# The final sums of a decoder step: sample rows moved to GpSimd, residual rows of two tiles put into TensorE's banks, half of the reads issued from ScalarE

## The chip, the cores and the metric

The program runs on one core of a Trainium2 chip. The core has a matrix engine (TensorE, PE in the profile), a vector engine (VectorE, DVE), an activation engine (ScalarE, ACT), a general engine (GpSimd, POOL) and a queue engine (SyncE, SP), each with its own stream of instructions; they wait for one another only through semaphores. Sixteen DMA engines move data between the device memory (HBM) and the on-chip memory (SBUF); TensorE writes to eight banks of 128 x 512 floats (PSUM). The metric is the time of one execution on the device, in microseconds (us).

## The reference

One decoder layer over 512 prompt rows and 8 sample rows of width 1024: normalisation, input projection, a gated spatial unit beside dilated attention, output projection; then a mixture of experts, and a last normalisation. The part that the change touches is the end:

```
xp = xp + moe(rmsnorm(xp, ln2_g))      # 512 rows
xs = xs + moe(rmsnorm(xs, ln2_g))      # 8 rows
y_prompt = rmsnorm(xp, lnf_g)          # x / sqrt(mean(x^2) + 1e-6) * g
y_sample = rmsnorm(xs, lnf_g)
```

In `moe` each row goes to two experts of the 32; its result is the sum of the two expert rows, each times its gate.

## The kernel before, in words

The rows lie in five tiles: tiles 0 to 3 hold 128 prompt rows each, tile 4 (`NT - 1`) the 8 sample rows. Nothing plans the order: each engine's stream is written out by hand.

The experts run as a loop over 16 pairs of experts (`work`). GpSimd gathers the rows of a pair, TensorE multiplies, ScalarE and VectorE each copy half of the result, and GpSimd scatters it to `y2_dram` (`expert_rows`) in HBM, by an indirect DMA; `y_landed` counts the scatters that have landed. A second round of the loop stands in a branch that every engine passes and none takes here.

Then come the final sums. SP has by then put `x_end`, the residual rows, and `gain_end`, the last gain, on the chip (L607, L608). When all scatters have landed it reads, tile by tile in `READ_ORDER` (sample first), the first-choice and the second-choice expert rows into `rows` (L615, ten DMAs on one queue). The sums are made in `LAST_ORDER`, sample first:

- For the sample and for tiles 0 and 2, VectorE adds gate x row to the residual row, twice (L1482, L1484). For tiles 1 and 3 (`BY_PE`), TensorE multiplies the rows by diagonal matrices of gates into four banks (L1900), and VectorE adds the banks to the residual rows in halves (L1478).
- ScalarE squares each tile with a running sum over the row (L984), and takes the root (L747). The first root needs a table load.
- VectorE takes the reciprocal (L1492) and multiplies row, reciprocal and gain (L1493); `add_rows` of the next tile stands ahead of `final_norm` of a tile in its stream.
- SP writes each tile out when it is ready (L618), and waits for all.

Between the expert loop and the rows, TensorE runs 100 products without a use (`keep_on`, L1797).

L636 is another place, in the attention over cached keys: GpSimd multiplies keys by a query there, in tiles of 128 x 1536. L1019, L1091 and L1133 are passes of VectorE that run near it, each with two inputs: L1019 and L1091 have both in SBUF, L1133 has one in a bank. L643 is a masking pass of GpSimd with one input, and L883 a square of half a tile by ScalarE with a running sum, as in the change.

Of the kernel before, what the change touches and what calls it, by code (L numbers as in the profile page):

```python
# [77 lines left out]
def rows_of(t):  # L78
    return P if t < NT - 1 else NS
# [84 lines left out]
LAST_ORDER = [NT - 1, 0, 2, 1, 3]  # L164
BY_PE = (1, 3)
# [11 lines left out]
ROOM = [32 - 4 * (i + 1) for i, h in TASKS]  # L177

# [28 lines left out]
def build(nc, x_prompt, x_sample, cache_k, cache_v, ln1_g, w_in, sgu_g, sgu_wt, sgu_w, sgu_bt, sgu_b,  # L207
# [7 lines left out]
    with ExitStack() as ctx:  # L215
# [3 lines left out]
        def sem(name):  # L219
            return ctx.enter_context(nc.semaphore(name))  # L220
# [185 lines left out]
        zeroed = sem("zeroed")  # L406
        diags_set, rows_gated = sem("diags_set"), sem("rows_gated")
# [42 lines left out]
        def down_load(sp, j):  # L450
            sp.dma_start(places[j % SLOTS][:, 2], down_v[:, 2 * j:2 * j + 2, :]).then_inc(down_in[j % SLOTS], 16)

# [3 lines left out]
        def _(sp):  # L456
# [165 lines left out]
        def _(pool):  # L622
# [80 lines left out]
            with pool.If(more > 0):  # L703
                pool.wait_ge(tab_ready, 2)
                with pool.Fori(PAIRS, TOTAL - PAIRS + 1, PAIRS) as base:
                    work(base)
            for s_, n_ in ((out_k, 32), (out_v, 32), (out_s, 16)):
                pool.wait_ge(s_, n_)

        @block.scalar  # L710
        def _(act):
# [269 lines left out]
            for i, t in enumerate(LAST_ORDER):  # L981
                n = rows_of(t)
                act.wait_ge(mixed, i + 1)
                nc.scalar.activation(hflat[0:n, 0:D], x_end[0:n, t, :], ACT.Square, scale=D ** -0.5,  # L984
                                     accum_out=stat[0:n, 24 + t:25 + t]).then_inc(sq3, 1)
                root(sq3, i + 1, stat[0:n, 24 + t:25 + t])

        @block.vector
        def _(dve):
# [431 lines left out]
            step(V.tensor_tensor(gates[:, 1, :], gates[:, 0, :], ex, ALU.mult))  # L1421
# [46 lines left out]
            def add_rows(t):  # L1468

                n = rows_of(t)  # L1470
                xt = x_end[0:n, t, :]
                dve.wait_ge(x_back[t], 16)
                if t in BY_PE:
                    i = BY_PE.index(t)
                    dve.wait_ge(rows_gated, i + 1)
                    for half in range(2):
                        xh = xt[:, half * 512:(half + 1) * 512]
                        ins = V.tensor_tensor(xh, (acc, tp)[i][half][:, :], xh, ALU.add)  # L1478
                    ins.then_inc(mixed, 1)
                    return  # L1480
                dve.wait_ge(rows_in[t], 32)  # L1481
                step(V.scalar_tensor_tensor(out=xt, in0=rows[0:n, t, 0], scalar=gates[0:n, 0, t:t + 1], in1=xt,  # L1482
                                            op0=ALU.mult, op1=ALU.add))
                V.scalar_tensor_tensor(out=xt, in0=rows[0:n, t, 1], scalar=gates[0:n, 1, t:t + 1], in1=xt,  # L1484
                                       op0=ALU.mult, op1=ALU.add).then_inc(mixed, 1)

            def final_norm(i, t):
                n = rows_of(t)
                xt = x_end[0:n, t, :]
                dve.wait_ge(mixed, i + 1)  # L1490
                dve.wait_ge(rooted, 2 * NT + i + 1)  # L1491
                step(V.reciprocal(stat[0:n, 24 + t:25 + t], stat[0:n, 24 + t:25 + t]))  # L1492
                V.scalar_tensor_tensor(out=xt, in0=xt, scalar=stat[0:n, 24 + t:25 + t], in1=gain_end[0:n, :],  # L1493
                                       op0=ALU.mult, op1=ALU.mult).then_inc(y_ready, 1)

            add_rows(LAST_ORDER[0])
            for i in range(1, NT):
                add_rows(LAST_ORDER[i])
                final_norm(i - 1, LAST_ORDER[i - 1])
            final_norm(NT - 1, LAST_ORDER[NT - 1])  # L1500

        @block.tensor
        def _(pe):
# [390 lines left out]
            keep_on(100)  # L1894
            pe.wait_ge(diags_set, 2 * len(BY_PE))
            for i, t in enumerate(BY_PE):
                pe.wait_ge(rows_in[t], 32)
                for half in range(2):
# [59 lines left out]
```

## Time and profile before

| | us |
|---|---|
| median of 3 runs | 441.01 |
| lowest, highest | 438.19, 441.26 |
| span of the profiled execution | 437.3 |
| VectorE busy | 214.6 (49%) |
| ScalarE busy | 150.9 (34%) |
| GpSimd busy | 70.5 (16%) |
| TensorE busy | 397.0 (91%) |

The span is the time from the first to the last instruction of one profiled execution; for that execution there is no other time. The three runs are whole executions, without a profile. Busy times are averages over the whole program; what matters for the change is its last 26 us, from the landing of the last scatter on, and which wait ends last there.

### The profile page before, as it was taken

How to read it: one execution, taken by the hardware profiler on the slowest of the kernel's cores; microseconds unless marked ns; L12 is line 12 of the kernel's file. 1: busy time of each engine (PE TensorE's matmuls, PEld its weight loads, DVE VectorE, ACT ScalarE, POOL GpSimd, SP SyncE). 2: the span in 40 equal slices, each digit the busy share in tenths (PEclk: the TensorE clock that was granted, in tenths of full speed). 3: DMA queues.
4: the chain of work that ended last, by engine and by line, in shares of the span. 5: the costliest groups of instructions: out<-in, count | busy, mean ns of one | idle time of the engine just before them, and what ended most of it. 6: DMA issues, size and time to landing. Idle time of an engine off the chain costs nothing. (4 is left out here: it accounts for less than half of the span.)

```text
span 437.3 us, 6404 instructions
## 1 busy us (share of the span) xinstructions
PE 397.0 (91%) x2466; PEld 211.0 (48%) x2466; DVE 214.6 (49%) x442; ACT 150.9 (34%) x321; POOL 70.5 (16%) x59
## 2 busy tenths in 40 slices
PE   1999998999799999999989998979999999999782
PEld 1454443443244434455533557756555555554551
DVE  2968345799597465455351525741222312222276
ACT  5724122132364455454332435211222312222043
POOL 0000113444350100000000000220323223211000
PEclk9999999899899999999999999788999999999897
DMA  8981530874935133940069994899999999994384
GB/s 290 357 245 49 194 96 0 305 273 135 328 117 194 42 101 124 302 157 1 6 222 411 411 414 174 257 375 396 338 409 414 410 410 407 403 402 169 125 332 192
DMA packets 42323, 109.17 MB, mean 250 GB/s; under 512 B 7864, under 2 KB 8632, under 8 KB 42288
## 3 DMA queue, kind: packets, MB, share of 16 engines
q1 hardware_dynamic: 36000, 94.79, 58.8%
q0 software_dynamic: 5856, 12.81, 7.8%
q10 hardware_dynamic: 432, 1.11, 0.8%
q8 instruction: 22, 0.36, 0.3%
q14 instruction: 13, 0.11, 0.1%
HBM read 100.00 MB, written 16.94 MB: 267 GB/s over the span
## 5 line engine op out<-in xcount | busy, mean ns | idle before, releaser
L1540 PE MATMUL bank<-weights_split,tokens_split 128*128 128x512 f16 (+1 forms) x648 | 151.2, 387 | 2.1 <-DVE x L1260 1.4
L1540 PEld LDWEIGHTS bank<-weights_split,tokens_split 128*128 128x128 f16 (+1 forms) x648 | 61.8, 98 | 81.1 <-issue 12.7
L636 POOL TENSOR_TENSOR big<-big,middle 128x1536 f32<-128x1536 f32 x8 | 27.8, 3469 | 93.9 <-DMA middle<-sample_q 52.3
L1848 PE MATMUL bank<-big,tokens_split 128*64 128x256 f32 x320 | 39.0, 399 | 1.6 <-ACT tokens_split L945 1.6
L1438 DVE TENSOR_TENSOR middle<-bank,middle 128x128 f32<-128x128 f32 x16 | 4.7, 293 | 59.2 <-ACT middle L950 59.2
L1848 PEld LDWEIGHTS bank<-big,tokens_split 128*64 128x64 f32 x320 | 23.9, 143 | 13.7 <-ACT tokens_split L945 2.1
L1019 DVE SCALAR_TENSOR_TENSOR weights_split<-middle,weights_split 128x1024 f16<-128x1024 f32 x16 | 20.8, 1333 | 12.8 <-ACT weights_split L738 12.7
L1797 PE MATMUL bank<-half_consts 128*128 128x256 f16 x186 | 23.8, 294 | 2.9 <-issue 2.9
L1515 PE MATMUL bank<-ident,big 128*128 128x128 f32 (+1 forms) x92 | 14.6, 295 | 12.7 <-DVE big L1029 9.3
L670 POOL DMA_INDIRECT tokens_split<-h_rows,middle x16 | 16.3, 1018 | 59.1 <-PE bank L1837 46.0
L822 ACT ACTIVATE middle<-bank 128x128 f32<-128x128 f32 (+3 forms) x32 | 13.9, 435 | 32.0 <-PE bank L1588 31.8
L1797 PEld LDWEIGHTS bank<-half_consts 128*128 128x128 f16 x186 | 19.3, 106 | 7.3 <-issue 3.8
L950 ACT ACTIVATE middle<-bank 128x128 f32<-128x128 f32 x16 | 4.5, 278 | 52.0 <-PE bank L1848 52.0
L683 POOL DMA_INDIRECT expert_rows<-weights_split,middle x16 | 16.1, 1004 | 38.5 <-DVE weights_split L1445 38.5
L652 POOL DMA_DIRECT2D h_rows<-middle x5 | 2.7, 537 | 121.4 <-ACT middle L912 121.4
L1540 PE MATMUL bank<-weights_split,big 128*128 128x512 f16 x96 | 22.0, 379 | 0.0
L1100 DVE CUSTOM_DVE_ANT_0 middle<-bank,big 128x128 f32<-128x128 f32 (+3 forms) x32 | 15.5, 486 | 12.2 <-PE bank L1580 12.0
L1445 DVE COPY weights_split<-bank 128x512 f32<-128x512 f32 x16 | 11.1, 692 | 20.3 <-PE bank L1867 17.7
L1837 PE MATMUL bank<-ident,tokens_split 128*128 128x128 f32 x128 | 18.1, 286 | 1.9 <-DMA tokens_split<-h_rows,middle 1.9
L1867 PE MATMUL bank<-big,middle 128*64 128x512 f32 x80 | 19.3, 604 | 0.6 <-ACT middle L955 0.6
L1515 PEld LDWEIGHTS bank<-ident,big 128*128 128x128 f32 (+1 forms) x92 | 11.0, 154 | 17.8 <-issue 11.8
L1588 PE MATMUL bank<-ident,middle 128*128 128x128 f32 x80 | 15.2, 288 | 4.1 <-DVE middle L1110 2.7
(199 smaller groups left out, 542.8 us busy)
## 6 DMA issues: line engine op xcount, KB each, us to landing
big<-in_w_gate SPq DMA_DIRECT2D x10, 1024.0 KB, 13.8
big<-in_w_up SPq DMA_DIRECT2D x10, 1024.0 KB, 17.5
big<-in_w_down SPq DMA_DIRECT2D x10, 1024.0 KB, 15.2
middle<-in_w_in SPq DMA_DIRECT2D x16, 512.0 KB, 6.6
big<-in_cache_win_k SPq DMA_DIRECT2D x24, 256.0 KB, 3.9
middle<-in_cache_win_v SPq DMA_DIRECT2D x24, 256.0 KB, 4.6
big<-in_w_out SPq DMA_DIRECT2D x8, 512.0 KB, 8.4
big<-expert_rows SPq DMA_DIRECT2D x8, 512.0 KB, 6.9
```

The source lines that it names most:

```text
L636: nc.gpsimd.tensor_tensor(prod[:, :, :], kring[:, b % 2], qb[:, b % 2, :].unsqueeze(1).to_broadcast([P, NPAT, W]), ALU.mult).then_inc(prod ...
L670: nc.gpsimd.indirect_dma_start(out=xg[:, b, :], out_offset=None, in_=h2_dram, in_offset=bass.IndirectOffsetOnAxis(ap=index, axis=0), bound ...
L683: nc.gpsimd.indirect_dma_start(out=y2_dram, out_offset=bass.IndirectOffsetOnAxis(ap=index, axis=0), in_=yrow[:, b, :], in_offset=None, bou ...
L1019: V.scalar_tensor_tensor(out=wg[:, n % 2, 1, 2 * i:2 * i + 2, :], in0=pieces(n)[i], scalar=W_UP, in1=wg[:, n % 2, 0, 2 * i:2 * i + 2, :], ...
L1100: V.tensor_tensor_reduce(out=sp_sb[:, n % 4, 0:width], in0=sbk[n % 2][:, 0:width], in1=mask[:, (3 - i) * P:4 * P], scale=-SCALE, scalar=3. ...
L1515: ins = T.transpose(tp[bank][:, c * m:(c + 1) * m], src, ident[0:m, 0:m])
L1540: ins = T.matmul(out, (hT if rows is None else rows)[:, high_low, k if rows is None else k - 4, tokens], wg[:, place, part, k, columns], s ...
L1588: ins = T.transpose(ptb[:, j * P:(j + 1) * P], sp_sb[:, n % 4, j * P:(j + 1) * P], ident[:, :])
L1797: T.matmul(sbk[1][:, 0:2 * P], before_h, half_consts[:, :, :], start=True, stop=True)
L1837: ins = T.transpose(sbk[k // 4][:, (k % 4) * P:(k % 4 + 1) * P], xg[:, b, k * P:(k + 1) * P], ident[:, :])
L1848: ins = T.matmul((ptb, ovb)[b][e * CAP:(e + 1) * CAP, 0:2 * FE], xT[:, b, k, e * CAP:(e + 1) * CAP], places[slot][:, 0:2, e, k * FE:(k + 1 ...
L1867: ins = T.matmul((acc, tp)[b][half][e * CAP:(e + 1) * CAP, :], hidT[:, b, e * CAP:(e + 1) * CAP], places[slot][:, 2, e, half * 512:(half + ...
```

## The change

The change touches only the final sums.

- The sample's part moves from VectorE to GpSimd: two products of row and gate (L722), two sums (L728), one product with the gain (L731) and one with the reciprocal (L734), each on 8 x 1024. ScalarE still squares and roots (L1022, L1025), VectorE still takes the reciprocal (`inverse3`, L1542).
- For tiles 1 and 3, TensorE first copies the residual rows into the banks, by a product with the identity (L1965), before the filler products, of which 70 are left; the gated rows are added onto them. VectorE's addition falls away. ScalarE squares the banks in halves and adds the two sums (`square3_banks`), and VectorE's norm reads the banks.
- The second-choice rows are read from ScalarE's queue, the first-choice rows still from SP's (`read_rows`, L463).
- The order is now sample, 0, 1, 2, 3. VectorE makes both sums of tiles 0 and 2 first, with the sample's reciprocal between them, and then the four norms.

VectorE's stream behind the expert loop, before (L1482 and L1484 are the two sums, L1478 the addition from the banks, L1492 and L1493 the norm; `rooted` counts ScalarE's roots):

```order
L1482 SCALAR_TENSOR_TENSOR big<-big,middle 8x1024 [waits rows_in4,x_back4,gain_back]
L1484 SCALAR_TENSOR_TENSOR big<-big,middle 8x1024 [waits vector_step]
L1482 SCALAR_TENSOR_TENSOR big<-big,middle 128x1024 [waits rows_in0,x_back0]
L1484 SCALAR_TENSOR_TENSOR big<-big,middle 128x1024 [waits vector_step]
L1492 RECIPROCAL stat<-stat 8x1 [waits rooted,mixed]
L1493 SCALAR_TENSOR_TENSOR big<-big,stat 8x1024 [waits vector_step]
L1482 SCALAR_TENSOR_TENSOR big<-big,middle 128x1024 [waits rows_in2,x_back2]
L1484 SCALAR_TENSOR_TENSOR big<-big,middle 128x1024 [waits vector_step]
L1492 RECIPROCAL stat<-stat 128x1 [waits rooted,mixed]
L1493 SCALAR_TENSOR_TENSOR big<-big,stat 128x1024 [waits vector_step]
L1478 TENSOR_TENSOR big<-bank0,big 128x512 [waits rows_gated,x_back1]
L1478 TENSOR_TENSOR big<-bank1,big 128x512
```

The same place with the change (L1534 and L1536 are the two sums, L1548 the norm of a tile in SBUF, L1553 that of a tile in banks):

```order
L1534 SCALAR_TENSOR_TENSOR big<-big,middle 128x1024 [waits rows_in0,x_back0,gain_back]
L1536 SCALAR_TENSOR_TENSOR big<-big,middle 128x1024 [waits vector_step]
L1542 RECIPROCAL stat<-stat 8x1 [waits rooted]
L1534 SCALAR_TENSOR_TENSOR big<-big,middle 128x1024 [waits rows_in2,x_back2]
L1536 SCALAR_TENSOR_TENSOR big<-big,middle 128x1024 [waits vector_step]
L1542 RECIPROCAL stat<-stat 128x1 [waits rooted]
L1548 SCALAR_TENSOR_TENSOR big<-big,stat 128x1024 [waits vector_step]
L1542 RECIPROCAL stat<-stat 128x1 [waits rooted]
L1553 SCALAR_TENSOR_TENSOR big<-bank0,stat,big 128x512 [waits vector_step]
L1553 SCALAR_TENSOR_TENSOR big<-bank1,stat,big 128x512
```

The sample's passes are gone from VectorE, except the reciprocal, which now stands ahead of the sums of tile 2.

ScalarE's stream at the same place, with the change (L1022 is the square of a tile in SBUF, L1025 the root, L1033 the square of a bank; the last two rows of a bank's tile add the halves and take the root):

```order
L463 DMA big<-expert_rows 8x1024 [waits y_landed1,y_landed0]
L463 DMA big<-expert_rows 128x1024 x4
L1022 ACTIVATE tokens_split,stat<-big 8x1024 [waits sample_mixed]
L1025 ACT_TABLE_LOAD
L1025 ACTIVATE stat<-stat,epsc 8x1 [waits sq3]
L1022 ACTIVATE tokens_split,stat<-big 128x1024 [waits mixed]
L1025 ACTIVATE stat<-stat,epsc 128x1 [waits sq3]
L1033 ACTIVATE tokens_split,stat<-bank0 128x512 [waits rows_gated]
L1033 ACTIVATE tokens_split,stat<-bank1 128x512
L1038 ACTIVATE stat<-stat,epsc 128x1 [waits sq3]
L1040 ACTIVATE stat<-stat 128x1 [waits sq3]
```

The first square, that of the sample, waits for GpSimd's second sum (`sample_mixed`) where it waited for VectorE (`mixed`); the five reads stand ahead of it.

GpSimd's stream behind its branch, which held nothing before:

```order
L722 TENSOR_TENSOR big<-big,middle 8x1024 [waits gates_ready,rows_in4,x_back4]
L722 TENSOR_TENSOR big<-big,middle 8x1024
L728 TENSOR_TENSOR big<-big 8x1024 [waits sample_gated]
L728 TENSOR_TENSOR big<-big 8x1024 [waits sample_mixed,sample_gated]
L731 TENSOR_TENSOR big<-big 8x1024 [waits sq3,gain_back]
L734 TENSOR_TENSOR big<-big,stat 8x1024 [waits sample_inverse,sample_gained]
```

All six are new there; the fifth waits for ScalarE's square, the sixth for VectorE's reciprocal.

The diff, cut to the code that the text speaks of:

```diff
-LAST_ORDER = [NT - 1, 0, 2, 1, 3]
-BY_PE = (1, 3)
+LAST_ORDER = [NT - 1, 0, 1, 2, 3]
+BY_PE, BY_VECTOR = (1, 3), (0, 2)
...
+def squared3(t):
+    return sum(3 if u in BY_PE else 1 for u in LAST_ORDER[:LAST_ORDER.index(t) + 1])
...
+        def read_rows(eng, t, k):
+            at, n = k * ROWS + t * P, rows_of(t)
+            eng.dma_start(rows[0:n, t, k], y2_dram[at:at + n, :]).then_inc(rows_in[t], 16)
...
             for t in READ_ORDER:
-                n = rows_of(t)
-                for k in range(2):
-                    at = k * ROWS + t * P
-                    sp.dma_start(rows[0:n, t, k], y2_dram[at:at + n, :]).then_inc(rows_in[t], 16)
-            for i, t in enumerate(LAST_ORDER):
-                sp.wait_ge(y_ready, i + 1)
+                read_rows(sp, t, 0)
+            for t in LAST_ORDER:
+                sp.wait_ge(sample_ready if t == NT - 1 else y_ready, max(t + 1 if t < NT - 1 else 1, 1))
...
+            xs_end = x_end[0:NS, NT - 1, :]
+            pool.wait_ge(x_back[NT - 1], 16)
+            pool.wait_ge(rows_in[NT - 1], 32)
+            pool.wait_ge(gates_ready, 1)
+            for k in range(2):
+                row = rows[0:NS, NT - 1, k]
+                nc.gpsimd.tensor_tensor(row, row, gates[0:NS, k, NT - 1:NT].to_broadcast([NS, D]),
+                                        ALU.mult).then_inc(sample_gated, 1)
+            for k in range(2):
+                pool.wait_ge(sample_gated, k + 1)
+                if k == 1:
+                    pool.wait_ge(sample_mixed, 1)
+                nc.gpsimd.tensor_tensor(xs_end, xs_end, rows[0:NS, NT - 1, k], ALU.add).then_inc(sample_mixed, 1)
+            pool.wait_ge(gain_back, 16)
+            pool.wait_ge(sq3, squared3(NT - 1))
+            nc.gpsimd.tensor_tensor(xs_end, xs_end, gain_end[0:NS, :], ALU.mult).then_inc(sample_gained, 1)
+            pool.wait_ge(sample_gained, 1)
+            pool.wait_ge(sample_inverse, 1)
+            nc.gpsimd.tensor_tensor(xs_end, xs_end, stat[0:NS, 24 + NT - 1:24 + NT].to_broadcast([NS, D]),
+                                    ALU.mult).then_inc(sample_ready, 1)
...
+            for b in range(2):
+                act.wait_ge(y_landed[b], 8 * PAIRS)
+            for t in READ_ORDER:
+                read_rows(act, t, 1)
...
+            def square3_banks(t):
+                i = BY_PE.index(t)
+                act.wait_ge(rows_gated, i + 1)
+                for half in range(2):
+                    nc.scalar.activation(hflat[:, half * 512:(half + 1) * 512], (acc, tp)[i][half][:, :], ACT.Square,
+                                         scale=D ** -0.5,
+                                         accum_out=stat[:, 64 + 2 * i + half:65 + 2 * i + half]).then_inc(sq3, 1)
+                act.wait_ge(sq3, squared3(t) - 1)
+                first, both = stat[:, 64 + 2 * i:65 + 2 * i], stat[:, 24 + t:25 + t]
+                nc.scalar.activation(first, first, ACT.Identity, bias=epsc[:, :]).then_inc(sq3, 1)
+                act.wait_ge(sq3, squared3(t))
+                nc.scalar.activation(both, stat[:, 65 + 2 * i:66 + 2 * i], ACT.Sqrt, bias=first).then_inc(rooted, 1)
...
-            add_rows(LAST_ORDER[0])
-            for i in range(1, NT):
-                add_rows(LAST_ORDER[i])
-                final_norm(i - 1, LAST_ORDER[i - 1])
-            final_norm(NT - 1, LAST_ORDER[NT - 1])
+                for half in range(2):
+                    at = slice(half * 512, (half + 1) * 512)
+                    ins = V.scalar_tensor_tensor(out=xt[:, at], in0=(acc, tp)[BY_PE.index(t)][half][:, :],
+                                                 scalar=stat[:, 24 + t:25 + t], in1=gain_end[:, at],
+                                                 op0=ALU.mult, op1=ALU.mult)
+                ins.then_inc(y_ready, 1)
+
+            add_rows(0)
+            inverse3(NT - 1).then_inc(sample_inverse, 1)
+            add_rows(2)
+            final_norm(0)
+            final_norm(1)
+            final_norm(2)
+            final_norm(3)
...
-            keep_on(100)
+            pe.wait_ge(y_a, PAIRS)
+            pe.wait_ge(y_d, PAIRS)
+            for i, t in enumerate(BY_PE):
+                pe.wait_ge(x_back[t], 16)
+                for half in range(2):
+                    T.matmul((acc, tp)[i][half][:, :], ident[:, :], x_end[:, t, half * 512:(half + 1) * 512],
+                             start=True, stop=False)
+            keep_on(70)
...
-                for half in range(2):
-                    for k in range(2):
+                for k in range(2):
+                    for half in range(2):
                         ins = T.matmul((acc, tp)[i][half][:, :], gate_diag[:, i, k], rows[:, t, k, half * 512:(half + 1) * 512],
-                                       start=k == 0, stop=k == 1)
+                                       start=False, stop=k == 1)
```

## Rows read from the trace of the kernel before

**Rows 1.** Chain that ended last, in order of time: start us, us, what
```profile
406.66 4.51 DMA expert_rows<-weights_split,middle
...
415.04 8.22 DMA big<-expert_rows
```

**Rows 2.** Timeline, VectorE: start us, us, engine line op out<-in xcount [idle <-releaser]
```profile
413.83 1.27 DVE L1482 SCALAR_TENSOR_TENSOR big<-big,middle 8x1024 f32<-8x1024 f32 x1 [8.04 <-DMA big<-expert_rows]
...
418.22 1.28 DVE L1482 SCALAR_TENSOR_TENSOR big<-big,middle 128x1024 f32<-128x1024 f32 x1 [1.80 <-DMA big<-expert_rows]
...
423.35 1.28 DVE L1482 SCALAR_TENSOR_TENSOR big<-big,middle 128x1024 f32<-128x1024 f32 x1 [1.15 <-DMA big<-expert_rows]
...
427.26 1.28 DVE L1478 TENSOR_TENSOR big<-bank,big 128x512 f32<-128x512 f32 x2
...
432.75 0.16 DVE L1492 RECIPROCAL stat<-stat 128x1 f32<-128x1 f32 x1 [0.23 <-ACT stat L747]
...
432.94 1.28 DVE L1493 SCALAR_TENSOR_TENSOR big<-big,stat 128x1024 f32<-128x1024 f32 x1
```

**Rows 3.** Timeline of the same stretch, ScalarE (ACT)
```profile
416.45 1.05 ACT L984 ACTIVATE tokens_split<-big 8x1024 f32<-8x1024 f32 x1 [10.76 <-DVE big L1484]
...
417.61 1.28 ACT L747 ACT_TABLE_LOAD   x1
...
418.91 0.29 ACT L747 ACTIVATE stat<-stat,epsc 8x1 f32<-8x1 f32 x1
...
420.86 1.06 ACT L984 ACTIVATE tokens_split<-big 128x1024 f32<-128x1024 f32 x1 [1.66 <-DVE big L1484]
...
422.04 0.29 ACT L747 ACTIVATE stat<-stat,epsc 128x1 f32<-128x1 f32 x1
```

**Rows 4.** Timeline of the same stretch, TensorE (PE) and SP's queue
```profile
407.44 12.76 PE L1797 MATMUL bank<-half_consts 128*128 128x256 f16 x100 [2.89 <-issue]
...
411.23 5.37 SPq L615 DMA_DIRECT2D big<-expert_rows  x10
...
420.82 3.67 PE L1900 MATMUL bank<-big,middle 128*128 128x512 f32 x8 [0.62 <-DMA big<-expert_rows]
...
425.77 3.70 PE L1900 MATMUL bank<-big,middle 128*128 128x512 f32 x8 [1.28 <-DMA big<-expert_rows]
```

**Rows 5.** Groups of instructions, GpSimd (POOL): busy us, mean ns | idle before
```profile
L643 POOL TENSOR_SCALAR_AFFINE_SELECT middle<-middle 128x1024 f32<-128x1024 f32 x1 | 1.3, 1259 | 0.0
```

**Rows 6.** Timeline of an earlier stretch, GpSimd and VectorE
```profile
89.28 0.67 DVE L1091 TENSOR_TENSOR middle<-big 8x512 f32<-8x512 f32 x1
...
89.51 3.73 POOL L636 TENSOR_TENSOR big<-big,middle 128x1536 f32<-128x1536 f32 x1 [4.92 <-DVE sT L1058]
...
96.88 3.44 POOL L636 TENSOR_TENSOR big<-big,middle 128x1536 f32<-128x1536 f32 x1 [3.63 <-DVE sT L1058]
...
98.66 0.69 DVE L1133 TENSOR_TENSOR big<-bank,middle 128x512 f32<-128x512 f32 x1
...
99.27 2.12 DVE L1019 SCALAR_TENSOR_TENSOR weights_split<-middle,weights_split 128x1024 f16<-128x1024 f32 x1
...
124.24 1.21 DVE L1019 SCALAR_TENSOR_TENSOR weights_split<-big,weights_split 128x1024 f16<-128x1024 f32 x1
```

**Rows 7.** Windows: length, busy us by engine, TensorE's clock, DMA share, GB/s
```profile
412.00:413.00 1.00, 1.00 (x12) 0.90 (x10) 0.00 (x0) 0.00 (x0) 0.00 (x0) 1.00 0.42 102
413.00:414.00 1.00, 1.00 (x11) 0.90 (x10) 0.17 (x1) 0.00 (x0) 0.00 (x0) 1.00 0.88 274
414.00:415.00 1.00, 1.00 (x11) 0.90 (x10) 1.00 (x1) 0.00 (x0) 0.00 (x0) 1.00 0.80 242
415.00:416.00 1.00, 1.00 (x11) 0.89 (x10) 0.96 (x2) 0.00 (x0) 0.00 (x0) 1.00 0.82 295
```

**Rows 8.** Timeline, ScalarE, a square of half a tile with its sum
```profile
249.94 0.60 ACT L883 ACTIVATE bank<-x 128x512 f32<-128x512 f32 x1
250.46 0.20 ACT L883 ACTIVATION_READ_ACCUMULATOR bank<-x 128x1 f32 x1
```

More of the change, by code:

```diff
@@ L406, in build @@
         zeroed = sem("zeroed")
+        gates_ready = sem("gates_ready")
+        sample_inverse, sample_mixed, sample_ready = sem("sample_inverse"), sem("sample_mixed"), sem("sample_ready")
+        sample_gated, sample_gained = sem("sample_gated"), sem("sample_gained")
         diags_set, rows_gated = sem("diags_set"), sem("rows_gated")
@@ L980, in _, with square3 @@
                     work(base)
-            for i, t in enumerate(LAST_ORDER):
+            for b in range(2):
+                act.wait_ge(y_landed[b], 8 * PAIRS)
+            for t in READ_ORDER:
+                read_rows(act, t, 1)
+            def square3(t):
                 n = rows_of(t)
-                act.wait_ge(mixed, i + 1)
+                if t == NT - 1:
+                    act.wait_ge(sample_mixed, 2)
+                else:
+                    act.wait_ge(mixed, BY_VECTOR.index(t) + 1)
                 nc.scalar.activation(hflat[0:n, 0:D], x_end[0:n, t, :], ACT.Square, scale=D ** -0.5,
                                      accum_out=stat[0:n, 24 + t:25 + t]).then_inc(sq3, 1)
-                root(sq3, i + 1, stat[0:n, 24 + t:25 + t])
+                act.wait_ge(sq3, squared3(t))
+                nc.scalar.activation(stat[0:n, 24 + t:25 + t], stat[0:n, 24 + t:25 + t], ACT.Sqrt,
+                                     bias=epsc[0:n, :]).then_inc(rooted, 1)
+            def square3_banks(t):
[8 more added lines that the diff above has]
+                nc.scalar.activation(first, first, ACT.Identity, bias=epsc[:, :]).then_inc(sq3, 1)
+                act.wait_ge(sq3, squared3(t))
+                nc.scalar.activation(both, stat[:, 65 + 2 * i:66 + 2 * i], ACT.Sqrt, bias=first).then_inc(rooted, 1)
+            for t in LAST_ORDER:
+                if t in BY_PE:
+                    square3_banks(t)
+                else:
+                    square3(t)
         @block.vector
@@ L1420, in _ @@
             step(V.reciprocal(gates[:, 0, :], gp))
-            step(V.tensor_tensor(gates[:, 1, :], gates[:, 0, :], ex, ALU.mult))
+            V.tensor_tensor(gates[:, 1, :], gates[:, 0, :], ex, ALU.mult).then_inc(gates_ready, 1)
+            dve.wait_ge(gates_ready, 1)
             dve.wait_ge(cnt_ready, 1)
@@ L1468, in add_rows @@
             def add_rows(t):
-                n = rows_of(t)
-                xt = x_end[0:n, t, :]
+                xt = x_end[:, t, :]
                 dve.wait_ge(x_back[t], 16)
-                if t in BY_PE:
-                    i = BY_PE.index(t)
-                    dve.wait_ge(rows_gated, i + 1)
-                    for half in range(2):
-                        xh = xt[:, half * 512:(half + 1) * 512]
-                        ins = V.tensor_tensor(xh, (acc, tp)[i][half][:, :], xh, ALU.add)
-                    ins.then_inc(mixed, 1)
-                    return
@@ L1481, in add_rows @@
[L1481 to L1494, printed above, removed]
@@ L1496, in _ @@
-            add_rows(LAST_ORDER[0])
-            for i in range(1, NT):
-                add_rows(LAST_ORDER[i])
-                final_norm(i - 1, LAST_ORDER[i - 1])
-            final_norm(NT - 1, LAST_ORDER[NT - 1])
+                dve.wait_ge(rows_in[t], 32)
+                step(V.scalar_tensor_tensor(out=xt, in0=rows[:, t, 0], scalar=gates[:, 0, t:t + 1], in1=xt,
+                                            op0=ALU.mult, op1=ALU.add))
+                V.scalar_tensor_tensor(out=xt, in0=rows[:, t, 1], scalar=gates[:, 1, t:t + 1], in1=xt,
+                                       op0=ALU.mult, op1=ALU.add).then_inc(mixed, 1)
@@ new lines, in inverse3, with final_norm @@
+            def inverse3(t):
+                v = stat[0:rows_of(t), 24 + t:25 + t]
+                dve.wait_ge(rooted, 2 * NT + LAST_ORDER.index(t) + 1)
+                return V.reciprocal(v, v)
+            def final_norm(t):
+                xt = x_end[:, t, :]
+                step(inverse3(t))
+                if t not in BY_PE:
+                    V.scalar_tensor_tensor(out=xt, in0=xt, scalar=stat[:, 24 + t:25 + t], in1=gain_end,
+                                           op0=ALU.mult, op1=ALU.mult).then_inc(y_ready, 1)
+                    return
+                for half in range(2):
[4 more added lines that the diff above has]
+                ins.then_inc(y_ready, 1)
@@ L1893, in _ @@
                     work(base)
-            keep_on(100)
+                pe.wait_ge(y_a, TOTAL)
+                pe.wait_ge(y_d, TOTAL)
+            pe.wait_ge(y_a, PAIRS)
[6 more added lines that the diff above has]
+            keep_on(70)
             pe.wait_ge(diags_set, 2 * len(BY_PE))
```

1 line of the change is left out of this document (removed).

## The prediction

> **What bounds the kernel now.** I read the chain that ended last first, then the timeline of its stretch engine by engine, then the groups of GpSimd. In the chain the reader should see that everything behind the expert loop is one string: the last scatter of expert rows lands at 411.17 us, the rows are read back, and from 415.04 to 423.25 the chain is the DMA that brings them in [rows 1]. VectorE takes the sample rows at 413.83, tile 0 at 418.22 (idle until its rows were there), tile 2 at 423.35 (again), and then works almost without a hole to its last norm, which ends at 432.94 + 1.28 = 434.22; the span ends at 437.3, when the last output has landed [rows 2]. ScalarE squares and roots each tile behind VectorE's sums and mostly waits [rows 3]. TensorE forms the gated rows of tile 1 from 420.82 and of tile 3 from 425.77, in 3.7 us each [rows 4]. So three things stand close together at the end: the landing of the rows, VectorE's 20 us of small work, and the order in which VectorE and ScalarE take the tiles.
>
> **The change part by part**
>
> *TensorE.* The identity products (four of the size of L1900's four, so about 3.7 us by [rows 4]) take the place of 30 of 100 filler products (12.76 us for 100, so 3.8 us). TensorE is then free at about 420, as before, when the rows of tile 1 land. Cost: nothing; its cover is the wait for those rows, and if that were gone, ScalarE's squares of tile 1 would be late, not VectorE. Its products for tile 3 end at 425.77 + 3.70 = 429.47 at the latest.
>
> *VectorE* loses the sample's three passes (1.27 each) and both pairs of L1478 (1.28 a pair), 6.4 us of busy time [rows 2]. The norms of tiles 1 and 3 read banks instead, in two halves; I take 1.28 for the pair, as for the pair of L1478, which reads the same banks.
>
> *ScalarE* takes tiles 1 and 3 in halves: 0.60 + 0.20 overlapped, 0.72 each [rows 8], then one more small step: 2 x 0.72 + 2 x 0.29 and gaps of 0.04 make 2.1 where a whole tile takes 422.33 - 420.86 = 1.5 [rows 3]. That is 1.2 more in all, and decides only if ScalarE ends last.
>
> *Second-choice rows from ScalarE's queue.* SP needs 5.37 us for ten issues [rows 4]; ScalarE is idle then. The engines that move the bytes are 0.88 busy at 413 and 0.82 at 415 [rows 7], so better feeding can bring rows at most about 1.1 us earlier (the idle shares from 412 to 416), and at the lower end not at all, or a little later for one tile. The Trainium skill (DMA: Bandwidth & Descriptors, "Issuing engines are not separate DMA queues") says that issuing from several engines saves the sequencer's issue time and nothing else; by it the gain would be 0.7 us or less. In my sum it is zero, because the landing no longer decides.
>
> *Sample rows on GpSimd.* Here is the sum. GpSimd does six two-input passes over 8x1024. Its only two-input row is L636, 128x1536 in 3.44 us [rows 6]; per element of a row that is 3.44 x 1024/1536 = 2.29 us a pass. No row shows it on eight partitions. Bounds: 1.26, the one-input pass over 1024 [rows 5], and 3.44, if the row's time were all fixed cost. I take 2.29: it is the same operation, and on VectorE eight rows cost what 128 do (1.27 against 1.28 [rows 2]). The Trainium skill (GPSIMD Engine Reference, "Performance versus the Vector engine") measured 4497 ns for 2048 elements, by which an estimate for 1024 is 2.25 and the sum 0.2 us smaller; its "Instruction dispatch" gives each core its own 16 partitions, so eight rows would not be quicker.
>
> *The two engines exclude each other.* A VectorE pass with two SBUF inputs that starts in a GpSimd pass waits for its end: L1019 from 99.27 took 2.12 instead of 1.21 and ended 1.07 after GpSimd's pass of 96.88 to 100.32. The other way round, GpSimd's pass of 89.51 took 3.73, because VectorE's L1091, on eight partitions, held on until 89.95. A VectorE pass with one input in a bank (L1133 at 98.66, 0.69) was not held [rows 6]. So VectorE's sums of tiles 0 and 2 and its norms of 0 and 2 alternate with GpSimd's passes; a pass that has waited costs 1.28 - 0.14 = 1.14 (the 0.14 from 1.21 against 1.07).
>
> *The string, on the time axis of the trace.* GpSimd starts at 413.8, when VectorE now does (its own branch, by TensorE's 2.89 us before L1797, could make it 414.1 [rows 4]). Two gate products to 418.38; tile 0's rows have landed; VectorE's first pass to 419.52; GpSimd's first sum to 421.81; VectorE's second pass to 422.95; GpSimd's second sum to **425.24**. Now ScalarE, whose list begins with the sample: square, table load and root took 416.45 to 419.20, 2.75 us [rows 3], so the root is there at 428.03. Behind it in ScalarE's queue wait the squares of tiles 0 to 3. VectorE stands at the sample's reciprocal meanwhile, with tile 2's sums behind it. GpSimd's gain product runs from the end of the square, 426.43, to 428.72; VectorE's first pass of tile 2 follows to 429.86, GpSimd's last product to 432.15, VectorE's second pass to 433.29. Then four norms, each 0.19 + 1.28 + 0.04 = 1.5: **439.3**. ScalarE has the roots of tile 0 at 429.5, tile 1 at 431.7, tile 2 at 434.8 and tile 3 at 437.0, each before its norm. SP waits for the sample first (432.2), which holds up no output.
>
> Against 434.22 that is **+5.1 us**. Put as one formula, the end is 425.6 + 6 x (one GpSimd pass): it is even with before at a pass of about 1.45 us, and 1% slower from 2.17. The profiled execution has a span of 437.3 and no other time; the runs have 438.19 to 441.26, median 441.01, so 0.9 to 4.0 lie around the span. I add the difference to the median: **446.1 us**.
>
> **Rivals**
>
> 1. *The exclusion does not bite*, for instance because eight rows share the port freely. Then the second sum ends at 413.8 + 4 x 2.29 = 422.96, the root at 425.75, VectorE's two passes of tile 2 at 428.55, four norms at 434.6: +0.4, 441.4 us. Against it: an eight-partition pass held GpSimd back [rows 6]. Chance 0.12.
>
> 2. *Faster, by a short GpSimd pass.* With 1.26 us the second sum is done at 418.84, the sample's root at 421.6, before tile 2's rows (423.25); nothing waits for GpSimd any more. Tile 3's rows then decide: TensorE to 429.47, ScalarE's 2.1 to 431.6, the norm to 433.1, which is -1.1; with rows up to 1.1 earlier -2.2: 438.8 to 439.9 us. It decides from a pass under 1.45. For it: no row shows GpSimd on eight partitions. Against it: the price by L636. Chance 0.15.
>
> 3. *Still slower.* A pass costs more than in proportion, up to 3.44, each 0.1 us of it 0.6 us at the end, or GpSimd comes late out of its branch: up to +12, 453 us. Chance 0.12.
>
> My forecast has the rest, 0.61. Inside it the ends are 444.9 (GpSimd keeps the port through its first three passes, and one VectorE pass goes out of the way of the second sum) and 447.5 (later start, pass of 2.4).
>
> **How the numbers follow.** The range 439.8 to 448.6 takes in the forecast with its ends, rival 1, the lower half of the cost in rival 3 and a little under half of rival 2: about 0.8. About 1% (4.4 us) is what a measurement of this kernel can tell from no change. Slower by more than that: most of the forecast (0.48) and most of rival 3 (0.1), 0.57 with rounding. Faster by over 1% needs an end below 429.8; even rival 2 falls short, so 0.05 for what the runs' own spread could do. The rest, 0.38, is within 1%.
>
> **What would show it.** In the profile after: six GpSimd passes of about 2.3 us, the last sum ending near 425 (419 for rival 2, 423 for rival 1); VectorE's sums of tiles 0 and 2 lengthened to 2 or 3 us each, ending where a GpSimd pass ends; ScalarE's square of the sample at 425 with tile 0's behind the table load; VectorE's last norm near 439; TensorE's products for tile 3 ending by 429.5 and their result waiting. The prediction is wrong if the GpSimd passes are under 1.5 us, if VectorE's sums keep 1.28 beside them, or if ScalarE's first square comes before 421.

## The result, and the profile after

The change makes the kernel slower by 0.85%: the ratio to the kernel before is 1.0085, with a 95% interval of 1.0054 to 1.0116. In the twelve runs of each that stand behind it the medians are 440.97 and 437.75 us (the three runs shown ahead of the prediction, with 441.01, are three of the twelve), so the ratio is some 3.7 us of 437.75, between 2.4 and 5.1. The profiled execution of the changed kernel took 443.11 us, its span is 441.4.

One profile and another differ by microseconds ahead of the part that was changed (the last scatter lands between 404.9 and 413.3 us in the eleven profiles), so I compare the last stretch alone: **the tail**, from the landing of the last scatter to the end of the span. Before it was 437.3 - 411.17 = 26.1 us; after, the last scatter lands at 408.29 + 4.06 = 412.35, and the tail is 29.0. So +2.9 us, inside the interval. The forecast was +5.1, the right way and too much. As a time it was 446.1, and 440.97 was measured: 3.3 us of that gap are the base to which the +5.1 was added, 441.01 from three runs where twelve have 437.75; the other 1.9 are the size of the change, 5.1 for the 3.2 between the two medians.

The chain that ended last, of the changed kernel (start us, us, what); of before it stands in [rows 1]:

```profile
408.29 4.06 DMA expert_rows<-weights_split,middle
...
412.43 2.65 DMA big<-expert_rows
...
415.21 3.74 POOL big L722 x2
418.95 2.31 POOL big L728
...
421.40 3.16 POOL big L728
...
424.58 1.15 ACT tokens_split L1022 x2
...
425.75 1.28 ACT L1025
...
427.45 2.19 DVE big L1534
...
429.66 2.79 DVE big L1536
...
432.56 1.28 DVE big L1548
```

Before, the chain lay on the DMA that brings the rows until 423.25. Now it leaves the DMA with the sample's rows, 2.9 us after the scatter, and never comes back to it: GpSimd's four passes, ScalarE's square, table load and root of the sample, VectorE's two passes of tile 2, and the norms.

The timeline of the same stretch shows who held whom; these rows answer to [rows 2 to 4]:

```profile
409.35 5.37 PE L1965 MATMUL bank<-big,ident 128*128 128x512 f32 x8 [2.85 <-issue]
412.42 3.62 SPq L463 DMA_DIRECT2D big<-expert_rows  x5
412.43 3.70 ACTq L463 DMA_DIRECT2D big<-expert_rows  x5
...
418.92 5.63 POOL L728 TENSOR_TENSOR big<-big 8x1024 f32<-8x1024 f32 x2
418.96 3.38 DVE L1534 SCALAR_TENSOR_TENSOR big<-big,middle 128x1024 f32<-128x1024 f32 x1 [11.53 <-DMA big<-expert_rows]
...
422.38 3.26 DVE L1536 SCALAR_TENSOR_TENSOR big<-big,middle 128x1024 f32<-128x1024 f32 x1
424.58 1.06 ACT L1022 ACTIVATE tokens_split<-big 8x1024 f32<-8x1024 f32 x1 [17.25 <-POOL big L728]
...
426.19 2.35 POOL L731 TENSOR_TENSOR big<-big 8x1024 f32<-8x1024 f32 x1 [1.65 <-ACT tokens_split L1022]
426.72 3.70 PE L1973 MATMUL bank<-big,middle 128*128 128x512 f32 x8 [0.93 <-DMA big<-expert_rows]
...
427.37 0.15 DVE L1542 RECIPROCAL stat<-stat 8x1 f32<-8x1 f32 x1 [1.74 <-ACT stat L1025]
427.45 2.18 DVE L1534 SCALAR_TENSOR_TENSOR big<-big,middle 128x1024 f32<-128x1024 f32 x1
...
428.62 2.75 POOL L734 TENSOR_TENSOR big<-big,stat 8x1024 f32<-8x1024 f32 x1
...
429.66 2.79 DVE L1536 SCALAR_TENSOR_TENSOR big<-big,middle 128x1024 f32<-128x1024 f32 x1
...
430.21 0.29 ACT L1040 ACTIVATE stat<-stat 128x1 f32<-128x1 f32 x1
...
436.86 1.41 DVE L1553 SCALAR_TENSOR_TENSOR big<-bank,stat,big 128x512 f32<-128x512 f32 x2
```

VectorE's four sums, 1.28 each before, take 3.38, 3.26, 2.18 and 2.79, and each ends about 1.1 after a GpSimd pass has ended: the first ends at 422.34, GpSimd's first sum at 418.95 + 2.31 = 421.26. Tile 3's products are done at 430.42, and their result waits until ScalarE takes it, behind tile 2, at 433.87.

### The profile page after: what moved, and what is told of

The parts are those of the page before. It is cut to its first block and busy times, and to the rows that moved or that the text cites. A ratio compares the mean times of both kernels' runs of the same rounds, so it can differ in the third digit from the quotient of the medians.

```text
span 441.4 us, 6365 instructions
## 1 busy us (share of the span) xinstructions
PE 396.4 (90%) x2444; PEld 208.7 (47%) x2444; DVE 215.0 (49%) x437; ACT 151.3 (34%) x327; POOL 84.8 (19%) x65
## 3 DMA queue, kind: packets, MB, share of 16 engines
q10 hardware_dynamic: 1024, 3.24, 2.0%
## 5 line engine op out<-in xcount | busy, mean ns | idle before, releaser
L1604 PEld LDWEIGHTS bank<-weights_split,tokens_split 128*128 128x128 f16 (+1 forms) x648 | 61.7, 98 | 81.6 <-issue 13.3
L1912 PEld LDWEIGHTS bank<-big,tokens_split 128*64 128x64 f32 x320 | 24.3, 145 | 14.0 <-ACT tokens_split L974 2.1
L1579 PE MATMUL bank<-ident,big 128*128 128x128 f32 (+1 forms) x92 | 14.6, 294 | 12.7 <-DVE big L1089 9.4
L1901 PEld LDWEIGHTS bank<-ident,tokens_split 128*128 128x128 f32 x128 | 14.4, 145 | 10.5 <-issue 5.8
L1861 PE MATMUL bank<-half_consts 128*128 128x256 f16 x156 | 19.1, 286 | 0.0
```

The costliest lines, as they stand in the source:

```text
L1579: ins = T.transpose(tp[bank][:, c * m:(c + 1) * m], src, ident[0:m, 0:m])
L1604: ins = T.matmul(out, (hT if rows is None else rows)[:, high_low, k if rows is None else k - 4, tokens], wg[:, place, part, k, columns], s ...
L1861: T.matmul(sbk[1][:, 0:2 * P], before_h, half_consts[:, :, :], start=True, stop=True)
L1901: ins = T.transpose(sbk[k // 4][:, (k % 4) * P:(k % 4 + 1) * P], xg[:, b, k * P:(k + 1) * P], ident[:, :])
L1912: ins = T.matmul((ptb, ovb)[b][e * CAP:(e + 1) * CAP, 0:2 * FE], xT[:, b, k, e * CAP:(e + 1) * CAP], places[slot][:, 0:2, e, k * FE:(k + 1 ...
```

## The experiments

The theory: the sample's chain on GpSimd costs the time, by its length, by holding VectorE and being held, and by standing first in ScalarE's list. The rivals: the other parts of the change cost it (two queues, identity products), or GpSimd's passes are only long and the holding costs nothing. One table for all. Every time is from that run's profile, counted from the landing of its last scatter, and the ratio is to the kernel before. In every run but e6 the difference of its tail from the tail before lies inside the interval of its ratio.

| | second sum of the sample | last norm | tail | ratio (95%) |
|---|---|---|---|---|
| before | 5.2 | 23.05 | 26.1 | 1 |
| the change | 12.2 | 25.9 | 29.0 | 1.0085 (1.0054 to 1.0116) |
| e1 sample on VectorE | 5.3 | 20.6 | 23.7 | 0.994 (0.9903 to 0.9977) |
| e2 only the sample on GpSimd | 12.0 | 28.1 | 31.2 | 1.0121 (1.0081 to 1.016) |
| e3 one queue | 12.0 | 25.7 | 28.9 | 1.006 (1.0019 to 1.0102) |
| e4 reciprocal later | 12.0 | 23.5 | 28.1 | 1.0068 (1.0035 to 1.0102) |
| e5 sums read a bank | 11.3 | 22.8 | 26.0 | 0.9989 (0.9952 to 1.0027) |
| e6 no gate products | 7.5 | 23.0 | 26.1 | 0.9935 (0.9895 to 0.9976) |
| e7 as e1, one queue | 5.2 | 21.3 | 24.3 | 0.9954 (0.9921 to 0.9988) |
| e8 as e1, idle passes | 5.4 | 25.8 | 29.0 | 1.0054 (1.0018 to 1.009) |
| e9 products with full operand | 13.1 | 26.6 | 29.7 | 1.0071 (1.004 to 1.0102) |

**e1, the sample back on VectorE.** GpSimd's six passes are taken out, and VectorE's list is:

```diff
-            add_rows(0)
-            inverse3(NT - 1).then_inc(sample_inverse, 1)
+            add_rows(NT - 1)
+            add_rows(0)
+            final_norm(NT - 1)
             add_rows(2)
```

> The whole change, but the sample's sums, gain and norm are back on VectorE (sums first, its norm between the sums of tiles 0 and 2). Counted from the landing of the last scatter to the end of the span, the kernel before took 26.1 us and the changed one 29.0. Theory (the sample's chain on GpSimd is the cost): nothing waits for GpSimd any more, the rows of tile 3 decide; their products end 18.1 us after the scatter, ScalarE needs 2.0, VectorE 1.5, the output 3.1: 24.8, 0.3% faster than before. Rival (the reads from two queues or the identity products cost the time): it stays near 29.

Measured: a tail of 23.7, 0.6% faster than before. So the other parts of the change gain, and the sample on GpSimd costs 5.3 us of tail (29.0 against 23.7). The chain is back on the rows of tile 3; a timeline of three engines:

```profile
425.93 3.70 PE L1953 MATMUL bank<-big,middle 128*128 128x512 f32 x8 [0.18 <-DMA big<-expert_rows]
...
429.67 0.60 ACT L1010 ACTIVATE tokens_split<-bank 128x512 f32<-128x512 f32 x1 [0.59 <-PE bank L1953]
...
431.83 1.41 DVE L1532 SCALAR_TENSOR_TENSOR big<-bank,stat,big 128x512 f32<-128x512 f32 x2
```

Products, squares, norm follow one another without a wait between. The tail came out 1.1 below what I expected, because tile 3's products began 13.3 us after the scatter where I had counted with 14.4, as in the changed kernel. This version beats both others.

**e2, only the sample's move.** The kernel before, with GpSimd's six passes from the change, and VectorE's list without the sample but for its reciprocal:

```diff
-            add_rows(LAST_ORDER[0])
-            for i in range(1, NT):
+            add_rows(LAST_ORDER[1])
+            dve.wait_ge(rooted, 2 * NT + 1)
+            V.reciprocal(stat[0:NS, 24 + NT - 1:24 + NT], stat[0:NS, 24 + NT - 1:24 + NT]).then_inc(sample_inverse, 1)
+            for i in range(2, NT):
```

> The kernel before with only the sample moved to GpSimd: one queue for the reads, no identity products, VectorE adds the banks of tiles 1 and 3 itself. Theory: slower than the change as a whole, since VectorE has 2.6 us more to do behind the sums of tile 2: about 31.5 us from the scatter to the end, 1.2% above before. Rival (queue or identity cost the time): near 26.

Measured: 31.2 and 1.0121, as the theory has it. Against e1's result this is the whole picture from the other side: the sample's move alone makes the tail 5.1 us longer, the rest of the change takes 2.2 off again (31.2 to 29.0).

**e3, one queue for the reads.**

```diff
-            for t in READ_ORDER:
-                read_rows(act, t, 1)
...
                 read_rows(sp, t, 0)
+                read_rows(sp, t, 1)
```

> The whole change, but all ten reads of expert rows from SP's queue. Theory: the landing does not decide, 29.0 us from the scatter to the end as with the change, tile 0's rows landing 0.4 us later. Rival (two queues feed the DMA engines better, and that matters): up to 1 us longer. Rival (two queues disturb each other): shorter.

Measured: 28.9, and the intervals of the ratios overlap widely. In the changed kernel the queue makes no difference that shows.

**e5, VectorE's sums read a bank.** This takes away what makes the two engines hold each other, with the amount of work kept:

```diff
-                step(V.scalar_tensor_tensor(out=xt, in0=rows[:, t, 0], scalar=gates[:, 0, t:t + 1], in1=xt,
-                                            op0=ALU.mult, op1=ALU.add))
...
+                for k in range(2):
+                    for half in range(2):
+                        at = slice(half * 512, (half + 1) * 512)
+                        ins = V.scalar_tensor_tensor(out=xt[:, at], in0=(ptb, ovb)[half][:, :], scalar=gates[:, k, t:t + 1],
+                                                     in1=rows[:, t, k, at], op0=ALU.mult, op1=ALU.add)
...
```

> The whole change, but VectorE's sums of tiles 0 and 2 read the residual operand from a bank (two halves of 512 a pass) and not from SBUF, which leaves out the residual rows and the first choice of these tiles; the length of the work is kept (four passes of 0.69 for two of 1.28). Theory with exclusion: these passes are not held by GpSimd and don't hold it; GpSimd's second sum is done 1 us earlier, tile 2's sums end about 3 us earlier, the last norm 3 us earlier: 26 us from the scatter to the end. Rival (GpSimd's passes are only long, the holding costs nothing): 28 to 29.

Measured: 26.0 and 0.9989. The timeline:

```profile
415.87 4.82 POOL L728 TENSOR_TENSOR big<-big 8x1024 f32<-8x1024 f32 x2
416.19 2.85 DVE L1537 SCALAR_TENSOR_TENSOR big<-bank,middle,big 128x512 f32<-128x512 f32 x4 [12.03 <-DMA big<-expert_rows]
...
423.51 0.15 DVE L1546 RECIPROCAL stat<-stat 8x1 f32<-8x1 f32 x1 [4.47 <-ACT stat L1025]
423.60 2.85 DVE L1537 SCALAR_TENSOR_TENSOR big<-bank,middle,big 128x512 f32<-128x512 f32 x4
...
424.76 1.88 POOL L734 TENSOR_TENSOR big<-big,stat 8x1024 f32<-8x1024 f32 x1
```

VectorE's sums run beside GpSimd's at their own length, 2.85 for four halves, and GpSimd's two sums take 4.82 together instead of 5.63. GpSimd still has the same six passes and the sample still stands first in ScalarE's list; yet the loss is gone. The rival that the length alone costs it falls: the holding is worth 3.0 us of tail, as much as the whole loss against the kernel before. Of the 5.3 us against e1, 2.3 remain, and VectorE stands 4.47 us at the sample's reciprocal here: that remainder I put down to the length of the chain, by this row and not by a run of its own.

**e8, passes that nobody waits for.** The counter-proof: e1, and three sums on GpSimd over memory that is not used again.

```diff
+            pool.wait_ge(rows_in[0], 32)
+            for i in range(3):
+                nc.gpsimd.tensor_tensor(x[0:NS, 2 + i, :], x[0:NS, 0, :], x[0:NS, 1, :], ALU.add).then_inc(sample_gained, 1)
```

> The version with the sample on VectorE (23.7 us from the last scatter to the end of the span), and three sums of 8x1024 on GpSimd that start when tile 0's rows have landed, on memory that nobody reads; no engine waits for them. Theory (two-input passes of the two engines hold each other): VectorE's passes over tile 0, the sample's norm and tile 2 are held, in whatever order the port is given, by three passes of 2.3 us less what fits into VectorE's idle 1 us; about 5 us later, 28 to 29 us. Rival (only the waiting for GpSimd's results costs): 23.7, no change.

Measured: 29.0, 5.3 us above e1, without a single wait for GpSimd's results.

```profile
417.92 8.92 POOL L718 TENSOR_TENSOR x<-x 8x1024 f32<-8x1024 f32 x3 [11.13 <-DMA big<-expert_rows]
417.94 3.41 DVE L1516 SCALAR_TENSOR_TENSOR big<-big,middle 128x1024 f32<-128x1024 f32 x1 [2.12 <-DMA big<-expert_rows]
...
421.38 3.25 DVE L1518 SCALAR_TENSOR_TENSOR big<-big,middle 128x1024 f32<-128x1024 f32 x1
...
424.73 3.19 DVE L1531 SCALAR_TENSOR_TENSOR big<-big,stat 8x1024 f32<-8x1024 f32 x1
```

Three GpSimd passes need 3 x 2.34 = 7.0 alone and took 8.92: two VectorE passes went in between. The third VectorE pass, on eight rows, was held as long as those on 128. So the two engines take turns at each boundary, even between GpSimd passes that stand back to back. The run shows that holding alone can cost this much, not that it costs 5.3 in the change, where e5 has 3.0 for it.

**e6, no gate products.**

```diff
-            for k in range(2):
-                row = rows[0:NS, NT - 1, k]
-                nc.gpsimd.tensor_tensor(row, row, gates[0:NS, k, NT - 1:NT].to_broadcast([NS, D]),
-                                        ALU.mult).then_inc(sample_gated, 1)
```

> The whole change, but GpSimd's two gate products are left out (the sample's expert rows are added ungated). Theory (the sample's chain sets the end): GpSimd's second sum is done 4.6 us earlier, 3.74 for the products and 0.9 for a hold that falls away; the end comes 3.8 us earlier, 25.2 us from the scatter to the end, since tile 3's rows then come close. Rival (the end is set by VectorE's own work): under 1 us earlier, 28 or more.

Measured: the second sum 4.7 us earlier, as expected, the tail 2.9 shorter, where 3.8 was expected. The rival (under 1 us) falls. The rows of this run, of its chain first:

```profile
401.99 2.92 DMA expert_rows<-weights_split,middle
...
406.51 11.31 DMA big<-expert_rows
...
417.81 1.88 POOL L729 TENSOR_TENSOR big<-big,stat 8x1024 f32<-8x1024 f32 x1 [1.30 <-DVE stat L1537]
417.92 2.86 DVE L1529 SCALAR_TENSOR_TENSOR big<-big,middle 128x1024 f32<-128x1024 f32 x1 [0.25 <-DMA big<-expert_rows]
```

Here GpSimd's last product started 0.11 us before VectorE's first pass of tile 2, and held it for 1.8. So the end hangs on tile 2's rows, which landed at 417.82, and on one more hold. How much the products cost is not settled: the last scatter took 2.92 us from its start to its landing here, 4.06 to 4.90 in the ten other profiles, so this tail begins early. Counted from the scatter's start the run is 4.1 us shorter than the change (29.0 for 33.1), and by the ratios (0.9935 for 1.0085) some 6.5. The chain's length counts; by these three measures the products cost between 2.9 and 6.5.

**e4, the sample's reciprocal behind the sums of tile 2.**

```diff
             add_rows(0)
-            inverse3(NT - 1).then_inc(sample_inverse, 1)
             add_rows(2)
+            inverse3(NT - 1).then_inc(sample_inverse, 1)
```

> The whole change, but VectorE takes the sample's reciprocal behind the sums of tile 2 and not ahead of them. Theory: VectorE's 1.74 us of waiting at the reciprocal fall away, but its first pass of tile 2 now comes into the way of GpSimd's gain product, and GpSimd's last product into the way of the norm of tile 0: 0.3 to 1.9 us earlier, 27.1 to 28.7 us. Rival (the queue at the reciprocal is the main cost, without holds): the full 1.74 or more.

Measured: a tail of 28.1 and 1.0068, not to be told apart from the change by time. The last norm ends 2.4 us earlier, more than the theory gave. The rival's figure (1.74 or more) fits, but not its condition that nothing is held:

```profile
424.47 1.27 DVE L1534 SCALAR_TENSOR_TENSOR big<-big,middle 128x1024 f32<-128x1024 f32 x1
...
425.11 2.85 POOL L731 TENSOR_TENSOR big<-big 8x1024 f32<-8x1024 f32 x1 [1.65 <-ACT tokens_split L1022]
425.78 3.26 DVE L1536 SCALAR_TENSOR_TENSOR big<-big,middle 128x1024 f32<-128x1024 f32 x1
```

VectorE's wait at the reciprocal was a part of the loss, and one hold fell away with it: the first pass of tile 2 now stands ahead of GpSimd's gain product and takes 1.27, not 2.18. But the tail is only 0.9 shorter. SP's queue shows where the rest went:

```profile
432.26 0.30 SPq L627 DMA_DIRECT2D out_y_sample<-big  x1
432.61 2.92 SPq L627 DMA_DIRECT2D out_y_prompt<-big  x4
```

SP waits for the sample ahead of all others. The norm of tile 0 was done at 430.5, but no tile could leave before 432.6, and then all four, 2 MB, were issued within 2.9 us (4.8 with the change), ending 4.7 us after the last norm; with the change it is 3.1, and 3.0 to 3.2 in the nine other profiles. Of the 2.4 us, 1.6 were turned into a wait for the output. In the changed kernel itself the sample went out at 431.40 and tile 0 at 433.88, so there it holds up nothing, as forecast.

No run moved the sample in ScalarE's list, so that part of the theory stays unshown. In the change the roots of tiles 0 and 1 were done by 430.50, and VectorE came to the norm of tile 0 only at 432.56: apart from the sample's own root, for which VectorE waited 1.74 us, no wait of VectorE for ScalarE shows there.

**e7, e1 with one queue.** The edit is that of e3.

> The version with the sample on VectorE, but all ten reads from SP's queue: of the change only the identity products, the squares and norms from banks and the order are left. Theory: here the landing of tile 3 decides, so the queue counts: with two queues its products began 13.3 us after the scatter, with one 14.6 before; up to 1.3 us longer, 24 to 25 us. Rival (issuing from two queues saves nothing that counts): 23.7.

Measured: 24.3 against e1's 23.7; by time (0.9954 and 0.994) they can't be told apart. Tile 3's products began 420.66 - 406.69 = 14.0 us after the scatter, 13.3 in e1, 14.6 before. In single profiles the second queue is worth 0.6 us where the landing decides. The landings move by that much from profile to profile, so I leave its share open. The Trainium skill (DMA: Bandwidth & Descriptors, "Issuing engines are not separate DMA queues") allows only the sequencer's issue time for it; these runs are no argument against that.

```profile
420.66 3.70 PE L1949 MATMUL bank<-big,middle 128*128 128x512 f32 x8 [1.28 <-DMA big<-expert_rows]
```

**e9, products with a full operand.**

```diff
+            pool.wait_ge(gain_back, 16)
...
-                nc.gpsimd.tensor_tensor(row, row, gates[0:NS, k, NT - 1:NT].to_broadcast([NS, D]),
+                nc.gpsimd.tensor_tensor(row, row, gain_end[0:NS, :],
```

> The whole change, but GpSimd's two gate products multiply by the full rows of the gain instead of by one gate spread over the row, so the sample's sum is wrong and the work has the same count. Theory (a GpSimd pass with two full operands takes 2.3 us, one with a spread operand 1.87, and that is what the forecast missed): the two products take 4.65 instead of 3.74 us, tile 0's rows land inside the second, VectorE's first pass gets the port ahead of the first sum; the second sum ends about 14.1 us after the last scatter (12.2 with the change), and the end comes about 2 us later, 31 us from the scatter. Rival (the length is by operation, not by operand): products 3.74 again, 29.0 us.

Measured: half of it.

```profile
416.15 4.65 POOL L723 TENSOR_TENSOR big<-big 8x1024 f32<-8x1024 f32 x2 [6.61 <-DMA big<-expert_rows]
...
420.77 5.62 POOL L729 TENSOR_TENSOR big<-big 8x1024 f32<-8x1024 f32 x2
421.58 2.61 DVE L1535 SCALAR_TENSOR_TENSOR big<-big,middle 128x1024 f32<-128x1024 f32 x1 [13.88 <-DMA big<-expert_rows]
```

The products take 4.65, so it is the operand that sets the price: one gate spread over the row makes a pass 0.45 us shorter than a full second row. But in this run tile 0's rows landed 8.3 us after the scatter (6.6 with the change, 7.05 before), again behind the products, so VectorE's first pass did not go ahead of the first sum. The second sum came at 13.1, not 14.1, and the tail at 29.7, not 31. By time (1.0071 and 1.0085) the two versions can't be told apart; what the run shows is the price of the passes.

## Why the prediction was right in kind and too large

**What held.** The mechanism, each piece of it in the trace. GpSimd's price per element on eight rows is close to that of L636 on 128: e5's two sums, which nothing held, took 2.34 each, against 2.29 worked out from L636, and the choice between 1.26 and 3.44 was right. The two engines exclude each other (e5, e8), and rival 1 falls: without the holding the tail is that of before (26.0 in e5). By numbers alone one would have taken rival 1: the time measured, 440.97, lies nearest to its 441.4, and the second sum, at 423.4 on the axis of before, nearest to its sign of 423. What refutes it are the lengths, 3.38 and 3.16 us where passes that nothing held take 1.28 and 2.34. VectorE stood 1.74 us at the sample's reciprocal, ScalarE's list waited behind the sample, TensorE's result for tile 3 waited. The gain product ended 4.0 us after the second sum, 0.5 later than by my sum. The reads from two queues and the identity products were not on the path that ended last.

**What failed**, in the order of my sum, was the size of two terms and the base. The forecast put the second sum of the sample 425.24 - 411.17 = 14.1 us after the last scatter; it came after 12.2. Two steps make that up:

- *"Two gate products to 418.38"*: I took 2.29 for every pass, from L636, whose second operand, a query of 512 values read three times over, runs along the row. The two products read one gate spread over the row, and took 3.74 together, not 4.58 (-0.84). The last product, with the spread reciprocal, is short as well (1.88 in e5). e9 shows that the operand is the cause.
- *"tile 0's rows have landed; VectorE's first pass to 419.52"*: I let VectorE's passes alternate with GpSimd's from the second product on. With the shorter products GpSimd's first sum began at 418.92, and VectorE's pass stood there at 418.96, 0.04 us later. So one hold of 1.14 fell out of the sample's chain. I had that case as the lower end, with another reason. This follows from the first miss: tile 0's rows came at 418.22 in the kernel before, ahead of 418.38, but not of the 417.54 that the shorter products give. In the four runs with the same six passes and sums (the change, e2, e3, e4) they landed behind the products each time, and the second sum ended 12.0 to 12.2 us after the scatter. With the longer products it would hang on the landing, 6.4 to 8.3 us after the scatter in the runs, a matter of tenths; e9's rows came too late to show it.

GpSimd's start was 0.2 later than counted (2.86 us after the scatter, for 2.63), and 0.1 of the -1.9 is left over. Behind the second sum it went another 0.4 quicker than counted (25.9 - 12.2 = 13.7, for 14.1), with the short last product in it, and against it 0.13 more for each pair of bank norms (1.41 for 1.28). Together -2.2, and 2.9 for 5.1.

The base is the third: *"I add the difference to the median"*, 441.01 of three runs, which lies 3.3 us above the median of twelve. With the size of the change too large, 0.57 went to slower by more than 1%; the 0.85% measured lies within 1%, which had 0.38. My estimate that about 1% can't be told from no change was too coarse as well: the interval begins at 0.54%.

A smaller miss stands in TensorE's part: the identity products took 5.37 us and not 3.7, at a granted clock of 0.5 to 0.7 from 410 to 414 (3.67 in e7, at 1.0), and the fillers ended 10 us after the scatter where before they ended at 9. It costs nothing here, as the tile's result waits anyway.

Rival 2's path, on which tile 3's rows decide, is not that of the change; e1 runs it: forecast there were -1.1 to -2.2, measured -2.4 (23.7 for 26.1). From the end of tile 3's products to the last norm it is 3.6 us in e1 and e7 and was 434.22 - 429.47 = 4.75 before, because VectorE no longer adds the banks; the rest is that the products start earlier.

Three figures of the prediction do not come out of its working, and none touches the result. The lower edge of the range, 439.8, takes in 0.1 us of rival 2's 438.8 to 439.9, not a little under half. The upper end 447.5 is 447.1 by its own terms (0.3 for the start, 6 x 0.11 for the pass). The 0.7 us for the second queue has no working; e1 and e7 differ by 0.6 in single profiles.

## What to carry to other kernels

Moving small work to an idle GpSimd is not free for VectorE: where both read two operands in SBUF, they took turns here, pass by pass, and a GpSimd pass on eight rows held VectorE for the whole of its 2.3 us. Price a moved step by the row of the same engine with the same kind of operands, a spread one included, and ask who stands behind its result in the lists of the other engines. If a change has several parts, work out each with the others taken away: here one part cost 5 us and the rest gained more than 2.

## What the runs showed of the hardware that I had not expected

- A two-input pass of GpSimd over 1024 elements takes 2.3 us with two full operands and 1.88 with one value spread along the row (L722, L734 in e5; e9). Per element, 2.28 ns on eight partitions (e5) stand beside 2.23 on 128 (L636, 3.43 us for 1536): fewer rows did not make it quicker.
- Between two back-to-back GpSimd passes a waiting VectorE pass gets in, and the other way round: strict turns (e8, where three GpSimd passes of 2.34 took 8.92). The Trainium skill (GPSIMD Engine Reference, "Specifications") names the shared interface and VectorE's passes with two SBUF inputs; these runs agree, and show that the unit of the exclusion is the whole pass.
- TensorE's granted clock, at its full level (2.4 GHz) until 410, was at or near the lower one (1.2 GHz) from there to 414, while the identity products ran; ahead of them TensorE had been idle for 2.85 us. Neither the products nor that idle stretch is shown to be the cause: in the kernel before the clock was at 0.50 from 408 to 411 under the filler products, and in e7 it stayed at 1.00 through the identity products, behind 2.87 us of idleness. Windows of the changed kernel, of before and of e7 (length, busy us of PE, PEld, DVE, ACT, POOL, clock, DMA share, GB/s), and e7's identity products:

```profile
411.00:412.00 1.00, 1.00 (x3) 0.47 (x2) 0.00 (x0) 0.00 (x0) 0.00 (x0) 0.50 0.05 16
...
409.00:410.00 1.00, 1.00 (x7) 0.74 (x5) 0.00 (x0) 0.00 (x0) 0.00 (x0) 0.50 0.03 4
...
405.00:406.00 1.00, 1.00 (x3) 0.39 (x3) 0.00 (x0) 0.00 (x0) 0.00 (x0) 1.00 0.04 8
...
403.46 3.67 PE L1941 MATMUL bank<-big,ident 128*128 128x512 f32 x8 [2.87 <-issue]
```
